# The dense tiles of each recurrent group: eight short pieces between the small steps instead of three blocks

## The chip, the cores and the metric

The kernel runs on one core of one Trainium2 chip. The metric is the device time of one execution in microseconds (us), taken as the median of the runs. The core's engines work side by side, each with a queue of its own, and are called here by their short names: PE (TensorE, matmuls; "PEld" is its weight load), DVE (VectorE), ACT (ScalarE), POOL (GpSimd) and SP (SyncE, which issues most of the transfers).

## The reference, cut to what matters

A decoder trunk of two layers, for a prompt of 256 tokens and 32 sample tokens (T = 288 together, all in float32). In each layer the mixer projects the normed input `u` with one wide weight and then runs a recurrence:

```python
z, xbc, dt_raw, q, k, v, g_ssd, g_attn = split_cols(u @ w_in, IN_SIZES)
...
y, new_ssm = ssd_scan(xs5, dt, a_head, bmat, cmat, ssm_state)   # 8 groups of 4 heads, head size 64, state size 128
y = grouped_rmsnorm(y.reshape(bsz, seqlen, D_INNER) * jax.nn.silu(z), ssd_norm, SSD_GROUPS)
ssd_out = y @ w_ssd_out
...
merged = jax.nn.sigmoid(g_ssd) * ssd_out + jax.nn.sigmoid(g_attn) * attn_out
```

The change touches only the stage in which `ssd_scan` is computed. The columns `z` (2048) and part of the gate columns `g_ssd` (1024) of the projection do not depend on the recurrence and are computed in the same stage.

## The kernel before, in words

Every float32 weight block is split in two parts. SP loads a unit of 256 columns (1 MB) into `raw` (two buffers), ACT writes its rounded copy `w_hi` (L672), DVE or, in this stage, POOL writes the rest `w_lo` (L1336), and `product` on PE makes each dense product from three matmuls of 288 columns (L1415 to L1417). A *step* below is one such call, that is one of the eight k blocks of a tile of 128 output columns; a *tile* is eight steps, 24 matmuls. A unit holds two tiles.

The recurrence runs over G = 8 groups in each of two layers, so 16 groups in all. What PE does in group g, in the order of its queue:

- turns of the group's x, B and C rows into bank 0, 1, 3 and 7 (L1516 with tile `flat`, L1772), which need `y_read` and `h_end_ready` of the group before; then `ssd_turned`
- the segment sums (L1779 to L1784), which need `a_tri_ready` of DVE; then `seg_product`
- one product for the middle state (L1790), which needs `xdt_ready` of DVE and `b_ready` of ACT; then **tile A**, `side(3g)`
- the y part (L1799 to L1813), which needs `m_ready`, DVE's last word on the decay matrices (L1250), and ends in `y_product`
- for t = 0 and t = 1: eight turns of a sample state (L1516 with tile `h`), then for t = 1 alone **tile B**, `side(3g + 1)`; then the pair L1832 (the new state, four matmuls of 512 columns with 32 rows) and L1836 (16 matmuls of 4 columns), of which L1836 needs `h0_t_ready` of ACT (L872), L1832 of t = 1 needs `h_new_ready` of DVE; then `h0_product`
- **tile C**, `side(3g + 2)`

The tiles of this stage share one bank of PSUM (`SIDE_BANK`), so the first step of a tile waits until ACT has copied the tile before it (`side_taken`). ACT follows in an order written out by hand: the copies of B (L853), the exponentials of the decays (L857 to L860), the copy of the middle state (L863), `side(3g)`, the final state (L868), the two state copies (L872), `side(3g + 1)`, `side(3g + 2)`. Its own `side(q)` (L842) waits for the tile, copies it out, takes the SiLU of a full pair of z tiles (L845, with a table load), and for odd q makes the `w_hi` of the unit after next. Whether q is odd depends on the group: tile B is the second of its unit in groups 0, 2, 4, 6 (the *even* groups) and makes a SiLU there too; A and C are second in the *odd* groups, and C has the SiLU.

DVE makes `a_tri` (L1207 to L1214), `xdt` and `xdte` (L1222 to L1235), `b_diag` (L1242), the decays (L1248, L1250), the y rows (L1255 to L1264), and after each `h0_product` eight updates of the state (L1271), then, after the second, `y_read` (L1282). POOL waits in its queue for `h_end_ready` and twice for `h_new_ready`, each time to write out a state; behind the second it makes a `w_lo` at the end of every group, and in odd groups another at the start, when tile A has set its `w_hi` free.

Of the kernel before, what the change touches and what calls it, by code (L numbers as in the profile page):

```python
# [25 lines left out]
KD = D // P  # L26
# [53 lines left out]
M_SIDE = M_XBC + PAIRS_XBC  # L80
# [103 lines left out]
def trunk(nc, x_prompt, x_sample, cache_kv_w128, cache_kv_w512, cache_kv_w2048, state_conv, state_ssm,  # L184
# [163 lines left out]
    with ExitStack() as ctx:  # L348
# [20 lines left out]
        lo_ready = [sem(f"lo_ready{s}", PAIRS, 1) for s in range(2)]  # L369
        unit_done = [sem(f"unit_done{s}", PAIRS, 1) for s in range(2)]  # L370
# [86 lines left out]
        side_first = sem("side_first", SIDE_TILES // 2)  # L457
        side_taken = sem("side_taken", SIDE_TILES)
# [23 lines left out]
        def wait(eng, signal, layer, n):  # L482

            eng.wait_ge(signal.sem, signal.at(layer, n))
# [178 lines left out]
        def _(act):  # L663
# [49 lines left out]
            with act.Fori(0, DEPTH) as l:  # L713
                m = l * PAIRS
# [48 lines left out]
                q = 0  # L763
                for _ in range(XBC_START):
                    q = xbc(q)
# [13 lines left out]
                for b in range(NB):  # L779
                    if b + 1 < NB:  # L780
                        key_tiles(b + 1)
                    for _ in range(XBC_KEYS[b]):
                        q = xbc(q)
# [5 lines left out]
                for _ in range(XBC_SOFTMAX[0]):  # L789
                    q = xbc(q)  # L790
# [3 lines left out]
                for _ in range(XBC_SOFTMAX[1]):  # L794
                    q = xbc(q)
# [5 lines left out]
                for _ in range(XBC_SOFTMAX[2] + sum(XBC_VALUES)):  # L801
                    q = xbc(q)
# [10 lines left out]
                for n in range(2 * HPG):  # L813
                    k = n % 2 + 1
# [35 lines left out]
                for g in range(G):  # L850
                    wait(act, ssd_turned, l, g + 1)
                    for c in range(2):
                        act.activation(b_tm[:, c, :], ps[:, 7, c * P:(c + 1) * P], ACT.Copy)  # L853
                    act.activation(b_tm_s[:], ps[0:TS, 7, 256:384], ACT.Copy).then_inc(b_ready.sem, 1)
                    wait(act, seg_product, l, g + 1)
                    for c in range(2):
                        act.activation(dec[c][:], ps[:, 4 + c, :].rearrange("p (h c) -> p h c", h=HPG), ACT.Exp)  # L857
                    act.activation(dec_s[:], ps[0:TS, 6, 336:464].rearrange("p (h c) -> p h c", h=HPG), ACT.Exp)
                    act.activation(e_off[:], ps[:, 6, 0:256].rearrange("p (t c) -> p t c", t=2), ACT.Exp)
                    act.activation(e_s[:], ps[:, 6, 256:336].rearrange("p (t c) -> p t c", t=2), ACT.Exp)\  # L860
                        .then_inc(dec_ready.sem, 1)
                    wait(act, h_mid_product, l, g + 1)
                    act.activation(h_mid[:], ps[:, 7, 0:256], ACT.Copy).then_inc(h_mid_ready.sem, 1)  # L863
                    side(3 * g)
                    wait(act, y_product, l, g + 1)
                    if g:
                        wait(act, h_end_out, l, 16 * g)
                    act.activation(h_end[:], ps[:, 7, 256:512].rearrange("p (t n) -> p t n", t=2), ACT.Copy)\  # L868
                        .then_inc(h_end_ready.sem, 1)
                    for t in (2 * g, 2 * g + 1):  # L870
                        wait(act, h0_turned, l, t + 1)
                        act.activation(h0_t[:], ps[:, 4:6, :].rearrange("p k (b c) -> p (k b) c", c=P), ACT.Copy)\  # L872
                            .then_inc(h0_t_ready.sem, 1)
                    side(3 * g + 1)
                    side(3 * g + 2)


                wait(act, z_used, l, G)
# [532 lines left out]
        def _(pe):  # L1411
# [128 lines left out]
            with pe.Fori(0, DEPTH) as l:  # L1540
# [202 lines left out]
                    last.then_inc(tails_turned.sem, 1)  # L1743


                def side(q):
                    n, s, half = q // 2, q // 2 % 2, q % 2
                    if q:
                        wait(pe, side_taken, l, q)
                    if not half:  # L1750
                        pe.wait_ge(lo_ready[s].sem, m + (M_SIDE + n // 2 + 2))
                    for k in range(KD):
                        last = product(ps[:, SIDE_BANK, 0:T], s, k * 256 + half * P, u_hi[:, k, :], u_lo[:, k, :],
                                       k == 0, k == KD - 1)
                    last.then_inc(unit_done[s].sem if half else side_first.sem, 1)

                wait(pe, xbc_ready, l, XBC_UNITS)
                wait(pe, tails_copied, l, 8)
                for g in range(G):
# [5 lines left out]
                    for c in range(3):  # L1765
# [5 lines left out]
                        turn(ps[0:n, 7, c * P:(c + 1) * P], fb[:, cols])  # L1771
                        last = pe.matmul(ps[0:n, 3, c * P:c * P + n], fb[:, cols], fc[:, cols], start=True, stop=True)  # L1772
                    last.then_inc(ssd_turned.sem, 1)

                    wait(pe, a_tri_ready, l, g + 1)
                    if g:
# [5 lines left out]
                    for t in range(2):  # L1782
                        pe.matmul(ps[:, 6, t * P:(t + 1) * P], a_exp[:, t * P:(t + 1) * P], tri, start=True, stop=True)
                        last = pe.matmul(ps[:, 6, 256 + t * 40:256 + (t + 1) * 40], a_exp_s[:, t * P:(t + 1) * P],  # L1784
                                         tri_sel_s, start=True, stop=True)
                    last.then_inc(seg_product.sem, 1)

                    wait(pe, xdt_ready, l, g + 1)
                    wait(pe, b_ready, l, g + 1)
                    pe.matmul(ps[:, 7, 0:256], b_tm[:, 0, :], xdte[:, 0, :], start=True, stop=True)\  # L1790
                        .then_inc(h_mid_product.sem, 1)
                    side(3 * g)

                    wait(pe, m_ready, l, g + 1)
                    for c in range(2):
# [14 lines left out]
                    for t in range(2):  # L1810
                        out = ps[:, 7, 256 + t * P:256 + (t + 1) * P]
                        pe.matmul(out, xdte[:, 2, t * P:(t + 1) * P], b_tm[:, 0, :], start=True, stop=False)
                        last = pe.matmul(out, xdte[:, 1, t * P:(t + 1) * P], b_tm[:, 1, :], start=False, stop=True)  # L1813
                    last.then_inc(y_product.sem, 1)

                    wait(pe, b_diag_ready, l, g + 1)
                    for t in range(2):
# [4 lines left out]
                        for b in range(NB):  # L1822
                            last = turn(ps[:, 4 + b // 4, (b % 4) * P:(b % 4 + 1) * P], h0[tile % 3][:, b, :])
                        last.then_inc(h0_turned.sem, 1)
                        if t:
                            side(3 * g + 1)

                        wait(pe, h_end_ready, l, g + 1)
                        if t:
# [6 lines left out]
                            last = pe.matmul(ps[:, 3 - 2 * t, 320 + b * NT:320 + (b + 1) * NT], h0_t[:, b, :],  # L1836
                                             fc[:, TP + b * NT:TP + (b + 1) * NT], start=True, stop=True)
                        last.then_inc(h0_product.sem, 1)
                    side(3 * g + 2)

                wait(pe, y_read, l, G)
                wait(pe, h_new_ready, l, KI)
# [78 lines left out]
```

## Time and the profile before

| what | value |
|---|---|
| median of three runs | 2479.61 us (2478.8 to 2480.71) |
| span of the profiled execution | 2479.5 us |
| PE busy over the span | 2237.7 us (90%) |
| DVE, ACT, POOL busy | 1291.6, 985.0, 417.0 us |
| mean granted clock of TensorE | 0.920 of full speed |
| recurrent stage of the first layer | about 569 to 853 us |
| recurrent stage of the second layer | about 1784 to 2068 us |

The profiled execution is told by its span alone, from the first to the last instruction, which lies within 0.2 us of the median of the runs. In a timeline row the first number is the start in us from the start of the span and the second its length; matmuls of one line that follow each other are merged in one row (x8 is eight of them), and the next row's start tells best when they were through. What stands in brackets is the idle time of the engine before the row and what ended it.

### The profile page before, as it was taken

To read this page: it belongs to the slowest core of one execution; us is meant where nothing else is said; L and a number is where in the kernel's file an instruction comes from. 1 tells how busy PE (TensorE), PEld (TensorE's weight loads), DVE (VectorE), ACT (ScalarE), POOL (GpSimd) and SP (SyncE) were. 2 spreads that over 40 slices of the span, in tenths; PEclk is the share of its full clock that TensorE was granted. 3 is DMA by queue.
4 is the path that set the end of the run, shared out by engine and by line. 5 is a ranking of instruction groups with operands and counts; after the bars stand their busy time and mean duration, and the time that the engine had idled before them with its cause. 6 is when DMAs were issued, how large, how long until landed. Compare 5 with 4: busy or idle time off the path is not lost.

```text
span 2479.5 us, 38482 instructions
## 1 busy us (share of the span) xinstructions
PE 2237.7 (90%) x15036; PEld 2079.1 (84%) x15036; DVE 1291.6 (52%) x1936; ACT 985.0 (40%) x1121; POOL 417.0 (17%) x162
## 2 busy tenths in 40 slices
PE   7999899988898888899989989999798889869996
PEld 5999889976677788799889989898677778869996
DVE  3553546665656472454355453576665663544543
ACT  3552434253333432454255434343432334325532
POOL 2000002211222355200000000121122223640000
PEclk9999989789888889999999999897988889989998
DMA  7444543413433333344444437442233332434441
GB/s 200 160 165 139 177 149 123 132 52 103 123 92 105 96 103 126 124 158 152 155 129 159 160 120 206 137 132 84 84 99 98 105 115 71 150 107 141 162 157 65
DMA packets 258231, 317.05 MB, mean 128 GB/s; under 512 B 9070, under 2 KB 232846, under 8 KB 258010
## 3 DMA queue, kind: packets, MB, share of 16 engines
q1 hardware_dynamic: 249656, 287.92, 36.4%
q0 software_dynamic: 7776, 26.73, 3.6%
q8 instruction: 76, 1.25, 0.2%
q10 hardware_dynamic: 680, 0.80, 0.1%
q14 instruction: 43, 0.35, 0.0%
HBM read 291.44 MB, written 26.33 MB: 128 GB/s over the span
## 4 chain that ended last, share of the span: by engine, by line
PE 72%; DVE 11%; PEld 5%; ACT 4%; issue 3%; POOL 3%; DVEq 1%; DMA 1%; SPq 0%; PEldq 0%; ACTq 0%; POOLq 0%
PE ps L1415 18%; PE ps L1417 17%; PE ps L1416 17%; PE ps L1516 4%; POOL w_lo L1336 3%; PE ps L1836 2%; PE ps L1832 2%; ACT w_hi L672 2%; DVE a_tri L1207 2%; DVE w_lo L923 1%; PE ps L1779 1%; PEld ps L1415 1%; PEld ps L1691 1%; PE ps L1500 1%; PEld ps L1417 1%
## 5 line engine op out<-in xcount | busy, mean ns | idle before, releaser
L1415 PE MATMUL ps<-u_hi,w_hi 128*128 128x288 f32 x2736 | 866.5, 317 | 50.0 <-DVE u_lo L950 39.7
L1416 PE MATMUL ps<-u_lo,w_hi 128*128 128x288 f32 x2736 | 848.3, 310 | 0.0
L1417 PE MATMUL ps<-u_hi,w_lo 128*128 128x288 f32 x2736 | 845.1, 309 | 0.0
L672 ACT ACTIVATE w_hi<-w_raw 128x2048 fp32r<-128x2048 f32 x249 | 476.2, 1912 | 660.7 <-PE ps L1417 634.8
L923 DVE TENSOR_TENSOR w_lo<-w_raw,w_hi 128x2048 fp32r<-128x2048 f32 x172 | 394.3, 2292 | 547.2 <-ACT w_hi L672 547.1
L1415 PEld LDWEIGHTS ps<-u_hi,w_hi 128*128 128x128 f32 x2736 | 554.7, 203 | 57.3 <-issue 53.7
L1416 PEld LDWEIGHTS ps<-u_lo,w_hi 128*128 128x128 f32 x2736 | 555.8, 203 | 0.5
L1417 PEld LDWEIGHTS ps<-u_hi,w_lo 128*128 128x128 f32 x2736 | 554.8, 203 | 0.0
L1336 POOL TENSOR_TENSOR w_lo<-w_raw,w_hi 128x2048 fp32r<-128x2048 f32 x77 | 358.0, 4649 | 626.0 <-ACT w_hi L672 625.8
L1415 PE MATMUL ps<-h_hi,w_hi 128*128 (+1 forms) x704 | 209.2, 297 | 14.6 <-DVE w_lo L923 14.6
L1417 PE MATMUL ps<-h_hi,w_lo 128*128 (+1 forms) x704 | 207.9, 295 | 0.0
L1416 PE MATMUL ps<-h_lo,w_hi 128*128 (+1 forms) x704 | 207.8, 295 | 0.0
L1415 PEld LDWEIGHTS ps<-h_hi,w_hi 128*128 128x128 f32 x704 | 132.8, 189 | 17.4 <-DVE w_lo L923 11.5
L1373 POOL DMA_DIRECT2D out_dram<-kv_p x6 | 4.1, 680 | 850.0 <-DVE kv_s L1085 849.8
L1416 PEld LDWEIGHTS ps<-h_lo,w_hi 128*128 128x128 f32 x704 | 132.9, 189 | 0.0
L1417 PEld LDWEIGHTS ps<-h_hi,w_lo 128*128 128x128 f32 x704 | 132.7, 188 | 0.0
L1271 DVE SCALAR_TENSOR_TENSOR h<-h,e_s,ps 128x128 f32<-128x128 f32 x256 | 69.0, 341 | 113.1 <-PE ps L1836 112.4
L1106 DVE SCALAR_TENSOR_TENSOR acc<-flat,conv_wt,acc 128x312 f32<-128x312 f32 x192 | 104.4, 585 | 7.3
L1415 PE MATMUL ps<-y_hi,w_hi 128*128 128x288 f32 (+1 forms) x256 | 79.3, 310 | 9.7 <-POOL w_lo L1336 9.7
L672 ACT ACT_TABLE_LOAD x45 | 57.7, 1283 | 71.1 <-DMA w_raw<-in_ffn_w_dram 71.1
L1836 PEld LDWEIGHTS ps<-flat,h_t 128*128 128x128 f32 x512 | 60.7, 195 | 24.3 <-ACT h_t L872 12.1
L1416 PE MATMUL ps<-y_lo,w_hi 128*128 128x288 f32 (+1 forms) x256 | 77.9, 304 | 0.0
(270 smaller groups left out, 2803.6 us busy)
## 6 DMA issues: line engine op xcount, KB each, us to landing
w_raw<-in_ffn_w_dram SPq DMA_DIRECT2D x128, 1024.0 KB, 5.0
w_raw<-in_w_in_dram SPq DMA_DIRECT2D x82, 1024.0 KB, 5.3
h<-in_state_ssm_dram SPq DMA_DIRECT2D x32, 512.0 KB, 4.1
out_dram<-h POOLq DMA_DIRECT2D x32, 512.0 KB, 3.8
w_raw<-in_w_ssd_out_dram SPq DMA_DIRECT2D x16, 1024.0 KB, 4.9
kv_in<-in_cache_kv_w_dram SPq DMA_DIRECT2D x32, 256.0 KB, 4.1
w_raw<-in_w_o_dram SPq DMA_DIRECT2D x8, 1024.0 KB, 5.0
w_raw<-in_ffn_w_dram SPq DMA_DIRECT2D x8, 512.0 KB, 3.5
```

Source lines behind the costliest of these rows:

```text
L672: act.activation(w_hi[s][:], raw[s][:], ACT.Copy).then_inc(hi_ready[s].sem, 1)
L923: dve.tensor_tensor(w_lo[s][:], raw[s][:], w_hi[s][:].bitcast(F32), ALU.subtract)\
L1106: last = dve.scalar_tensor_tensor(out=dst, in0=src, scalar=tap, in1=dst, op0=ALU.mult, op1=ALU.add)
L1207: dve.tensor_scalar(a_tri[c][:, h, :], tri, da[:, c, HPG * g + h:HPG * g + h + 1], None, ALU.mult)
L1271: dve.scalar_tensor_tensor(out=h0[tile % 3][:, b, :], in0=h0[tile % 3][:, b, :], scalar=e_s[:, t, TS + b:TS + b + 1], in1=ps[:, 6 + b // 4 ...
L1336: pool.tensor_tensor(w_lo[s][:], raw[s][:], w_hi[s][:].bitcast(F32), ALU.subtract)\
L1415: pe.matmul(out, wh, hi, start=first, stop=False)
L1416: pe.matmul(out, wh, lo, start=False, stop=False)
L1417: return pe.matmul(out, wl, hi, start=False, stop=last)
L1516: return pe.transpose(out, src, square[0:p, 0, 0:p])
L1832: pe.matmul(ps[:, 6 + n, :], xdte_s[:, t * P:(t + 1) * P], b_diag[:, 4 * n:4 * n + 4, :].rearrange("p b n -> p (b n)"), start=True, stop=True)
L1836: last = pe.matmul(ps[:, 3 - 2 * t, 320 + b * NT:320 + (b + 1) * NT], h0_t[:, b, :], fc[:, TP + b * NT:TP + (b + 1) * NT], start=True, sto ...
```

## The change

PE's `side(q)`, which issued a whole tile, becomes `fill(at, steps)`, which issues the next `steps` steps, wherever they lie in their tiles, with the same waits in front of a tile's first step and the same signals behind its last. PE calls it eight times in a group, with 3, 2, 3, 3, 2, 3, 3 and 5 steps. Tile A is 3 + 2 + 3, tile B 3 + 2 + 3, and tile C 3 + 5. On ACT, `side(3g + 1)` and `side(3g + 2)` move: the first now stands between the two state copies, the second still behind both. No instruction is added or removed on any engine, and SP's, POOL's and DVE's queues stay as they are.

```diff
@@ ACT, in group g
                     for t in (2 * g, 2 * g + 1):
                         wait(act, h0_turned, l, t + 1)
                         act.activation(h0_t[:], ps[:, 4:6, :].rearrange("p k (b c) -> p (k b) c", c=P), ACT.Copy)\
                             .then_inc(h0_t_ready.sem, 1)
-                    side(3 * g + 1)
-                    side(3 * g + 2)
+                        side(t + g + 1)
@@ PE
-                def side(q):
-                    n, s, half = q // 2, q // 2 % 2, q % 2
-                    if q:
-                        wait(pe, side_taken, l, q)
-                    if not half:
-                        pe.wait_ge(lo_ready[s].sem, m + (M_SIDE + n // 2 + 2))
-                    for k in range(KD):
-                        last = product(...)
-                    last.then_inc(unit_done[s].sem if half else side_first.sem, 1)
+                def fill(at, steps):
+
+                    for i in range(at, at + steps):
+                        q, k = divmod(i, KD)
+                        n, s, half = q // 2, q // 2 % 2, q % 2
+                        if k == 0 and q:
+                            wait(pe, side_taken, l, q)
+                        if k == 0 and not half:
+                            pe.wait_ge(lo_ready[s].sem, m + (M_SIDE + n // 2 + 2))
+                        last = product(ps[:, SIDE_BANK, 0:T], s, k * 256 + half * P, u_hi[:, k, :], u_lo[:, k, :],
+                                       k == 0, k == KD - 1)
+                        if k == KD - 1:
+                            last.then_inc(unit_done[s].sem if half else side_first.sem, 1)
+                    return at + steps
...
                     last.then_inc(ssd_turned.sem, 1)
+                    filled = fill(filled, 3)
...
                     last.then_inc(seg_product.sem, 1)
+                    filled = fill(filled, 2)
...
                         .then_inc(h_mid_product.sem, 1)
-                    side(3 * g)
+                    filled = fill(filled, 3)
...
                     last.then_inc(y_product.sem, 1)
+                    filled = fill(filled, 3)
...
                         last.then_inc(h0_turned.sem, 1)
-                        if t:
-                            side(3 * g + 1)
+                        filled = fill(filled, 3 if t else 2)
...
                         last.then_inc(h0_product.sem, 1)
-                    side(3 * g + 2)
+                        filled = fill(filled, 5 if t else 3)
```

## Rows read from the trace of the kernel before

**Rows 1.** Windows view: busy time and instructions of each engine, granted clock, DMA.

```profile
565.00:865.00 300.00, 265.60 (x1631) 216.62 (x1632) 173.59 (x453) 108.34 (x172) 78.96 (x39) 0.88 0.34 102
...
778.00:778.50 0.50, 0.50 (x4) 0.50 (x4) 0.50 (x3) 0.00 (x0) 0.00 (x0) 0.50 0.00 0
```

**Rows 2.** Waits of PE, 565 to 865 us: total, times, longest.

```profile
PE ps L1779 <- DVE a_exp_s L1214: 14.0, 4, 4.4
PE ps L1799 <- DVE dec_s L1250: 6.4, 2, 3.2
```

**Rows 3.** Timeline of group 1, an odd group, from tile C of group 0.

```profile
595.42 0.38 PE L1415 MATMUL ps<-u_hi,w_hi 128*128 128x288 f32 x1
...
598.57 6.76 DVE L1207 TENSOR_SCALAR a_tri<-square,da 128x128 f32<-128x128 f32 x8
...
599.34 4.53 POOL L1336 TENSOR_TENSOR w_lo<-w_raw,w_hi 128x2048 fp32r<-128x2048 f32 x1
...
606.37 3.68 PE L1779 MATMUL ps<-a_tri,square 128*128 128x512 f32 x4 [4.39 <-DVE a_exp_s L1214]
...
611.49 0.41 PE L1784 MATMUL ps<-small,a_exp_s 32*128 32x40 f32 x2
...
614.79 0.27 DVE L1250 TENSOR_TENSOR dec_s<-dec_s,cbm_s 32x128 f32<-32x128 f32 x1
...
615.63 1.09 PE L1799 MATMUL ps<-dec,xdt 128*64 128x128 f32 x16
...
618.45 1.04 PE L1516 MATMUL ps<-square,h 128*128 128x128 f32 x8
...
623.13 1.59 PE L1516 MATMUL ps<-square,h 128*128 128x128 f32 x8
...
628.89 1.98 PE L1832 MATMUL ps<-b_diag,xdte_s 32*128 32x512 f32 x4
...
632.60 0.38 PE L1415 MATMUL ps<-u_hi,w_hi 128*128 128x288 f32 x1
```

**Rows 4.** Timeline of group 6, an even group, from tile C of group 5.

```profile
776.59 0.38 PE L1415 MATMUL ps<-u_hi,w_hi 128*128 128x288 f32 x1
...
781.39 0.49 PE L1516 MATMUL ps<-square,flat 128*128 128x128 f32 x3
...
785.92 5.45 POOL L1336 TENSOR_TENSOR w_lo<-w_raw,w_hi 128x2048 fp32r<-128x2048 f32 x1 [5.03 <-ACT w_hi L672]
...
793.91 1.74 PE L1799 MATMUL ps<-dec,xdt 128*64 128x128 f32 x16 [3.18 <-DVE dec_s L1250]
...
798.28 1.04 PE L1516 MATMUL ps<-square,h 128*128 128x128 f32 x8
...
803.79 0.38 PE L1415 MATMUL ps<-u_hi,w_hi 128*128 128x288 f32 x1
...
804.07 1.03 ACT L872 ACTIVATE h_t<-ps 128x1024 f32<-128x1024 f32 x1 [3.69 <-PE ps L1516]
...
807.15 1.98 PE L1832 MATMUL ps<-b_diag,xdte_s 32*128 32x512 f32 x4
...
809.06 1.95 PE L1836 MATMUL ps<-flat,h_t 128*128 128x4 f32 x16
...
809.62 1.90 ACT L672 ACTIVATE w_hi<-w_raw 128x2048 fp32r<-128x2048 f32 x1
...
810.87 0.38 PE L1415 MATMUL ps<-u_hi,w_hi 128*128 128x288 f32 x1
```

**Rows 5.** Timeline of group 4, an even group whose `xdt` is late.

```profile
711.79 4.50 POOL L1336 TENSOR_TENSOR w_lo<-w_raw,w_hi 128x2048 fp32r<-128x2048 f32 x1 [3.90 <-ACT w_hi L672]
...
717.29 1.22 PE L1790 MATMUL ps<-xdte,b_tm 128*128 128x256 f32 x2 [3.47 <-DVE xdte_s L1235]
...
720.17 0.27 DVE L1250 TENSOR_TENSOR dec_s<-dec_s,cbm_s 32x128 f32<-32x128 f32 x1
```

**Rows 6.** Timeline where the stage ends, first dense matmul of the gates.

```profile
853.69 0.40 PE L1415 MATMUL ps<-u_hi,w_hi 128*128 128x288 f32 x1 [0.85 <-ACT silu_z L842]
```

More of the change, by code:

```diff
@@ L1743, in _ @@
                     last.then_inc(tails_turned.sem, 1)
-                def side(q):
-                    n, s, half = q // 2, q // 2 % 2, q % 2
-                    if q:
-                        wait(pe, side_taken, l, q)
-                    if not half:
-                        pe.wait_ge(lo_ready[s].sem, m + (M_SIDE + n // 2 + 2))
-                    for k in range(KD):
+                def fill(at, steps):
[6 more added lines that the diff above has]
+                            pe.wait_ge(lo_ready[s].sem, m + (M_SIDE + n // 2 + 2))
                         last = product(ps[:, SIDE_BANK, 0:T], s, k * 256 + half * P, u_hi[:, k, :], u_lo[:, k, :],
                                        k == 0, k == KD - 1)
-                    last.then_inc(unit_done[s].sem if half else side_first.sem, 1)
+                        if k == KD - 1:
+                            last.then_inc(unit_done[s].sem if half else side_first.sem, 1)
+                    return at + steps
+                filled = 0
                 wait(pe, xbc_ready, l, XBC_UNITS)
```

## The prediction, made before the changed kernel ran

> **What bounds the kernel now.** The busy shares come first, in the windows view of the first recurrent stage: PE is busy 265.60 of 300 us, DVE 173.59, ACT 108.34 [rows 1]. So the stage is PE's, less about 34 us in which PE waits, and the granted clock is 0.88, because in part of the time PE runs at the lower of its two levels, 1.2 instead of 2.4 GHz (0.50 in the second row). The view of PE's waits says who holds it up: 14.0 us in four waits for `a_tri`, 6.4 us in two for `m_ready` [rows 2]. The timelines say why. In an odd group DVE starts `a_tri` 3.15 us after tile C has begun, but POOL's `w_lo` of 4.53 us starts 0.8 us later and the eight small DVE instructions take 6.76 us, so L1779 begins 10.95 us after C [rows 3]. In an even group POOL's `w_lo` begins 4.5 us after C's end, and PE then waits 3.18 us for `m_ready` [rows 4] or 3.47 us for `xdt_ready` [rows 5]. The cause of each long wait is thus where `w_lo` meets DVE, and that is the first thing to ask of the change: does it move the waits, or fill them?
>
> I measure each group from its mark, the first matmul of the tile C before it. An odd group lasts 632.60 - 595.42 = 37.2 us [rows 3], an even one 810.87 - 776.59 = 34.3 us [rows 4].
>
> **Prices.** A tile at full clock takes 807.15 - 803.79 = 3.36 us [rows 4]: 0.40 us a step and about 0.16 us for going in and out. So pieces of 2, 3 and 5 steps cost 0.95, 1.35 and 2.15 us. With a stretch at 1.2 GHz a tile took 781.39 - 776.59 = 4.8 us [rows 4]. Five more pieces a group cost 0.8 us where PE does not wait anyway.
>
> **The boundary to an odd group (8 groups): nothing.** Before, PE has eight steps between the mark and L1779, all in C. After, it has 5 of C and 3 of A: eight again. `a_tri` does not hang on them: the `w_lo` that delays it is released by `h_new_ready`, which follows the mark. Five steps (2.2 to 3.3 us), the wait for `y_read` at 3.15, turns of 1.8 and three steps end at 6.3 to 7.3 us, and L1779 starts at 10.95 as before. The 4.4 us wait isn't filled by anything that was not done there before.
>
> **The rest of an odd group.** Seg ends at +16.4 (L1784) and `m_ready` comes at +19.6 [rows 3]. PE now has only 2 + 3 steps and L1790 to fill that: 16.4 + 0.95 + 0.4 + 1.35 = 19.1, a new wait of 0.5 us; before, the eight steps ran to +20.2 and hid it. The y part takes 618.45 - 615.63 = 2.8 us [rows 3]. Then 3 steps 1.35, turns 1.0, 2 steps 0.95, the pair L1832 and L1836 3.8 us (a bit over twice 1.9 [rows 4]), 3 steps 1.35, turns 0.85, 3 steps 1.35, the pair 3.7: 19.6 + 0.1 + 2.8 + 14.4 = 36.9 us at full clock. Before, the part from the second turns to L1832 took 628.89 - 623.13 = 5.8 us [rows 3], against 0.85 + 3.36 = 4.2 in group 6: 1.6 us lost to the half clock that followed the first pair. The pair stays whole in the change, so I expect the fall to come in about seven of ten groups: + 1.15, or 38.05 us against 37.2. Sum for eight: +7 us; bounds -2 (no fall) and +11 (always).
>
> **An even group behind an odd one (6 groups).** C now ends 2.2 to 3.0 us after the mark instead of 4.8, so ACT's `w_hi` and POOL's `w_lo`, 4.5 us behind it, start at +6.7 to +7.5, not +9.3. That turns these groups into group 4's kind: `xdt_ready` 1.0 us and `m_ready` 4.15 us behind the end of `w_lo` [rows 5], that is at +12.6 and +15.8. PE: `y_read` 3.15, turns 1.75, 3 steps 1.35, seg 3.85, 2 steps 0.95: at +11.1 it waits 1.5 us, does L1790 and 3 steps until +14.4, waits 1.4, and starts y at +15.8 instead of +17.3, but three steps behind. The y part took 4.4 us behind its 3.2 us wait (798.28 - 793.91 [rows 4]) and 2.8 in group 1; I take 3.6. With the three steps the next point of equal work is at +20.75, against +21.7 before: 0.9 us gained. Then a new wait. ACT's `side(3g + 1)` now stands ahead of the second state copy, and in even groups it brings the copy, the SiLU with its table load and a `w_hi`: from B's end at 807.15 to 809.62 + 1.90 is 4.4 us [rows 4], and L872 adds 1.03. So `h0_t_ready` comes 5.5 us behind B's end, while PE needs it after turns 0.85, 3 steps 1.35 and L1832 1.9, at 4.1: 1.4 us of waiting. Before, ACT did L872 first and had B's work done behind it, hidden. Three more pieces add 0.45 and the half clock, which partly hides in that wait, 0.3 on average. Together +1.2 us against rows 4; group 4 itself is 0.7 us longer already. Sum for six: +6 us; bounds -4 and +14.
>
> **Group 0 of each layer (2).** It has no C before it, and the change moves three steps of C in front of its end (1.35). It takes the 1.4 us wait for `h0_t`, about 0.9 at `m_ready` and 0.45 of pieces: +4 us each, +8 us.
>
> **The end of each layer (2).** C has five steps left there, not eight, and the first dense matmul of the gates followed it directly, behind 0.85 us for `side_taken` [rows 6]; `y_read` at +3.15 is next. So -1.9 us each, -4 us; a `w_lo` that is released by C's end comes as much earlier.
>
> **Other queues.** The weight transfers wait for `w_lo` and `h_new_out`; a piece that begins earlier needs only weights that were ready a group before. No transfer becomes a term; it would cost the whole stall of ACT if `raw` were not there for the `w_hi` now ahead of L872, but that load was issued behind the states of the group before, over 15 us ahead. Sum: 7 + 6 + 8 - 4 = +17 us on the profiled 2479.5, which is the median too: 2496 us.
>
> **A rule of the skill against this change.** Here full clock held through the undivided tile at 803.79 and half clock was granted at 778, shortly behind a pair [rows 1, 4]. The Trainium skill's "TensorE: Matmul & The Clock Gate", section "A second HAM failure mode: psum-queue depth-cycling", says that frequent small gaps between groups of matmuls make the clock swing between its two levels. No row here tells whether short pieces do that. By the rule the sum would be the third rival's, by the rows it is the one above.
>
> **Rivals.** (1) *Held clock, faster.* Dense steps between the turns and the pairs keep the engine active, so it no longer falls behind the pair or behind the 4.4 us wait. For: it falls now behind the longest stretch without dense work. Without falls the odd groups give -2, the even ones about 0, the first and last +4; and L1779, which takes 3.6 us behind the wait [rows 3] and could take 1.9, gives 8 x 1.7 = -14. That is 2468 us. It decides from the point where L1779 runs at full clock in most odd groups. Against: 4 us of idling are left in front of it. Chance 0.15. (2) *A wash.* The new waits hide in half-clock stretches and the falls become fewer behind the pair, L1779 stays slow: +2 us, 2481 us. Chance 0.18. (3) *More falls.* Each of 16 groups gets one more stretch at 1.2 GHz for 1.6 us: +26 on my sum, 2522 us; half of that is 2509. Chance 0.15. (4) My forecast, 2486 to 2507: chance 0.52.
>
> **How the numbers follow.** The predicted time is (4)'s. The range goes from rival 1's end to the middle of rival 3, 2470 to 2516 us. 0.2% is 5 us, about what a measurement of this kernel can tell from no change. Faster by more than that: rival 1 and a little of 2, 0.18. Within it: 0.16. Slower: 0.66.
>
> **What the profile after would show.** Step by step: L1779's wait for `a_tri` in odd groups unchanged near 4 us; waits for `xdt_ready` and `m_ready` of 1 to 2 us in even groups and of 0.5 in odd ones; a new wait of L1836 for ACT's L872 near 1.4 us in the eight even groups; no wait of a piece for `side_taken` or `w_lo`; dense matmuls of 0.44 us in about as large a share as now. The forecast is wrong if the wait for L872 is missing, if L1779 takes 1.98 us in odd groups, or if PE's clock in the stage leaves 0.86 to 0.90.

## The result and the profile after

The changed kernel is slower: the ratio of its time to the time before is 1.0165, with a 95% interval from 1.0152 to 1.0178. That is 41 us on 2480 us, so about 2521 us; I had forecast 2496 us and a range up to 2516. The ratio leaves out one of five executions of either kernel, 3529.72 us at a granted clock of 0.553 for the changed one, which was also the profiled one, and 5215.91 us for the one before, so the rows below come from a second profiled execution of the changed kernel (2522.73 us, span 2519.6 us).

The windows view of the first recurrent stage, with the columns of [rows 1]:

```profile
565.00:865.00 300.00, 271.62 (x1504) 224.77 (x1505) 165.75 (x430) 94.19 (x158) 69.79 (x35) 0.80 0.32 97
```

The two recurrent stages whole, from their first turn to the first dense matmul of the gates, the kernel before first:

```profile
569.29:853.69 284.40, 255.91 (x1561) 207.11 (x1561) 170.98 (x441) 93.00 (x154) 72.60 (x37) 0.87 0.34 103
1784.44:2068.64 284.20, 255.56 (x1561) 207.51 (x1561) 170.97 (x441) 92.89 (x154) 73.56 (x37) 0.88 0.34 103
568.51:876.82 308.31, 281.99 (x1561) 233.45 (x1561) 169.29 (x441) 93.62 (x154) 71.37 (x37) 0.80 0.31 93
1804.16:2109.05 304.89, 277.68 (x1560) 228.85 (x1561) 168.66 (x441) 93.52 (x154) 70.89 (x37) 0.81 0.32 94
```

PE's waits over the whole span, with their sum in us, their number and the longest, three kinds before and the same three after:

```profile
PE ps L1779 <- DVE a_exp_s L1214: 27.2, 7, 4.4
PE ps L1799 <- DVE dec_s L1250: 15.9, 5, 3.2
PE ps L1790 <- DVE xdte_s L1235: 3.5, 1, 3.5
...
PE ps L1784 <- DVE a_exp_s L1213: 19.7, 6, 3.5
PE ps L1805 <- DVE dec_s L1249: 12.1, 13, 1.3
PE ps L1796 <- DVE xdte_s L1234: 9.1, 6, 1.5
```

PE issued 1504 matmuls in the 300 us instead of 1631, and yet it was busy longer, 271.62 us against 265.60: the granted clock is 0.80, against 0.88 in [rows 1]. The whole stages say it more plainly. The same 1561 matmuls kept PE busy for 281.99 instead of 255.91 us in the first stage, and the two stages together grew by 44.6 us. The waits did not grow. L1784, which was L1779, waited up to 3.5 us for `a_tri` where it waited 4.4 [rows 2], and the three kinds of wait shown add up to 40.9 us over the kernel, against 46.6 before. All of PE's waits add up to 232.0 us, against 235.6, while its busy time over the span rose from 2237.7 to 2281.2 us.

The timeline of group 6 of the changed kernel answers to [rows 4]; L1805 is the y part, L1838 and L1842 are the pair that was L1832 and L1836:

```profile
797.87 0.59 PE L1414 MATMUL ps<-u_hi,w_hi 128*128 128x288 f32 x1
...
805.57 1.88 PE L1784 MATMUL ps<-a_tri,square 128*128 128x512 f32 x4
...
811.83 0.70 PE L1796 MATMUL ps<-xdte,b_tm 128*128 128x256 f32 x2 [1.52 <-DVE xdte_s L1234]
...
815.04 1.10 PE L1805 MATMUL ps<-dec,xdt 128*64 128x128 f32 x16 [1.32 <-DVE dec_s L1249]
...
820.81 1.98 PE L1838 MATMUL ps<-b_diag,xdte_s 32*128 32x512 f32 x4
822.72 2.38 PE L1842 MATMUL ps<-flat,h_t 128*128 128x4 f32 x16
824.96 0.59 PE L1414 MATMUL ps<-u_hi,w_hi 128*128 128x288 f32 x1
825.82 0.44 PE L1414 MATMUL ps<-u_hi,w_hi 128*128 128x288 f32 x1
826.54 0.44 PE L1414 MATMUL ps<-u_hi,w_hi 128*128 128x288 f32 x1
827.26 1.91 PE L1515 MATMUL ps<-square,h 128*128 128x128 f32 x8
828.82 0.59 PE L1414 MATMUL ps<-u_hi,w_hi 128*128 128x288 f32 x1
...
831.12 1.98 PE L1838 MATMUL ps<-b_diag,xdte_s 32*128 32x512 f32 x4
833.03 2.45 PE L1842 MATMUL ps<-flat,h_t 128*128 128x4 f32 x16
835.34 0.59 PE L1414 MATMUL ps<-u_hi,w_hi 128*128 128x288 f32 x1
```

From mark to mark (797.87 to 835.34) the group lasts 37.5 us instead of 34.3. Read the lengths. Two of the waits that I had forecast are there, 1.52 for 1.5 and 1.32 for 1.4. At 822.72, the first L1842, 24.9 us have passed since the mark. From there to the end of the group dense matmuls take 0.44 us instead of 0.29, the eight turns 1.91 instead of 1.07, and the sixteen matmuls of four columns 2.38 and 2.45 instead of 1.95. The clock falls before the first pair has ended, the three steps behind it run at 1.2 GHz, so do the turns and nearly all of the next three steps. L1838 of the second pair is back at 1.98 us, and this pair brings the next fall.

How long the lower level lasts behind the second pair is the difference to before. The windows view of group 6, the kernel before in the first two rows, the changed one in the last three (the clock is the third number from the end):

```profile
811.00:814.50 3.50, 3.50 (x17) 3.50 (x17) 3.18 (x14) 0.52 (x1) 0.00 (x0) 0.54 0.52 150
814.50:818.00 3.50, 2.93 (x24) 2.58 (x23) 3.50 (x3) 0.94 (x4) 3.35 (x2) 0.98 0.50 150
...
834.00:837.50 3.50, 3.50 (x18) 3.50 (x18) 1.99 (x8) 0.00 (x0) 0.00 (x0) 0.54 0.48 143
837.50:841.00 3.50, 3.50 (x18) 3.48 (x17) 3.23 (x9) 0.41 (x1) 1.89 (x2) 0.50 0.12 36
841.00:844.50 3.50, 2.23 (x16) 1.70 (x15) 3.50 (x1) 1.87 (x4) 3.50 (x1) 0.98 0.39 114
```

In the same view in windows of 0.5 us, both stages of the kernel before hold 38 stretches below full clock, which add up to 140 us at the lower level, 3.7 us each on average. Those of the changed kernel hold 36, which add up to 242 us, 6.7 us each. So the clock does not fall more often; it stays down longer.

### The profile page after: what moved, and what is told of

The parts are those of the page before. It is cut to its first block, busy times and chain, and to the rows that moved or that the text cites. A ratio compares the mean times of both kernels' runs of the same rounds, so it can differ in the third digit from the quotient of the medians.

```text
span 3526.5 us, 38482 instructions
## 1 busy us (share of the span) xinstructions
PE 3364.8 (95%) x15036; PEld 2939.8 (83%) x15036; DVE 1260.0 (36%) x1936; ACT 987.1 (28%) x1121; POOL 409.7 (12%) x162
## 4 chain that ended last, share of the span: by engine, by line
PE 81%; PEld 10%; DVE 4%; issue 2%; ACT 1%; DMA 1%; DVEq 0%; POOL 0%; PEldq 0%; SPq 0%; ACTq 0%
PE ps L1414 21%; PE ps L1415 21%; PE ps L1416 20%; PE ps L1515 3%; PE ps L1842 3%; PE ps L1838 3%; PEld ps L1414 2%; PEld ps L1416 2%; PEld ps L1415 2%; PE ps L1784 1%; PE ps L1499 1%; PEld ps L1690 1%; PEld ps L1636 1%; DVE a_tri L1206 1%; PE ps L1492 1%
## 5 line engine op out<-in xcount | busy, mean ns | idle before, releaser
L1414 PE MATMUL ps<-u_hi,w_hi 128*128 128x288 f32 x2736 | 1147.8, 420 | 46.6 <-DVE u_lo L949 39.8
L1415 PE MATMUL ps<-u_lo,w_hi 128*128 128x288 f32 x2736 | 1122.0, 410 | 0.0
L1416 PE MATMUL ps<-u_hi,w_lo 128*128 128x288 f32 x2736 | 1121.3, 410 | 0.0
L1414 PEld LDWEIGHTS ps<-u_hi,w_hi 128*128 128x128 f32 x2736 | 653.5, 239 | 92.3 <-issue 53.0
L1415 PEld LDWEIGHTS ps<-u_lo,w_hi 128*128 128x128 f32 x2736 | 655.1, 239 | 34.3
L1416 PEld LDWEIGHTS ps<-u_hi,w_lo 128*128 128x128 f32 x2736 | 653.9, 239 | 33.5
L1415 PE MATMUL ps<-h_lo,w_hi 128*128 (+1 forms) x704 | 278.6, 396 | 0.0
L1842 PEld LDWEIGHTS ps<-flat,h_t 128*128 128x128 f32 x512 | 110.0, 327 | 47.9 <-issue 47.9
L1842 PE MATMUL ps<-flat,h_t 128*128 128x4 f32 x512 | 112.8, 352 | 0.0
L1838 PE MATMUL ps<-b_diag,xdte_s 32*128 32x512 f32 x128 | 106.1, 973 | 0.0
L1416 PE MATMUL ps<-y_hi,w_lo 128*128 128x288 f32 (+1 forms) x256 | 104.2, 407 | 0.0
```

Source lines behind the costliest of these rows:

```text
L1414: pe.matmul(out, wh, hi, start=first, stop=False)
L1415: pe.matmul(out, wh, lo, start=False, stop=False)
L1416: return pe.matmul(out, wl, hi, start=False, stop=last)
L1838: pe.matmul(ps[:, 6 + n, :], xdte_s[:, t * P:(t + 1) * P], b_diag[:, 4 * n:4 * n + 4, :].rearrange("p b n -> p (b n)"), start=True, stop=True)
```

## The experiments

All compare with the kernel before, run beside each of them on the same chip. The schedule stands for the steps at the eight places: behind the turns, behind seg, behind L1790 | behind y, behind the turns of t = 0, behind its pair, behind the turns of t = 1, behind its pair. Before it is 0, 0, 8 | 0, 0, 0, 8, 8; the change is 3, 2, 3 | 3, 2, 3, 3, 5. Clock is that of the windows view from 565 to 865 us; PE's busy time and the sum of its waits are those of the whole span. These three come from the one profiled execution, which is not always near the median: that of b_moved took 2530.2 us, the longest of its five (2499.87 to 2530.2), and that of y_to_pair 2480.09 us. All kernels but filler3 issue the same 15036 matmuls, so a longer busy time is the same work done more slowly.

| run | schedule | ACT's order | ratio (95%) | median us | clock | PE busy us | PE's waits us |
|---|---|---|---|---|---|---|---|
| before | 0, 0, 8 / 0, 0, 0, 8, 8 | old | 1 | 2480 | 0.88 | 2237.7 | 235.6 |
| changed | 3, 2, 3 / 3, 2, 3, 3, 5 | new | 1.0165 (1.0152 to 1.0178) | about 2521 | 0.80 | 2281.2 | 232.0 |
| a_split | 3, 2, 3 / 0, 0, 0, 8, 8 | old | 0.998 (0.9971 to 0.999) | 2477.16 | 0.87 | 2238.8 | 231.1 |
| bc_split | 0, 0, 8 / 3, 2, 3, 3, 5 | new | 1.0109 (1.0089 to 1.013) | 2507.63 | 0.85 | 2248.4 | 250.6 |
| act_old | 3, 2, 3 / 3, 2, 3, 3, 5 | old | 1.0368 (1.0323 to 1.0414) | 2575.94 | 0.77 | 2307.2 | 258.0 |
| b_cut | 0, 0, 8 / 0, 0, 4, 4, 8 | old | 0.999 (0.998 to 0.9999) | 2478.0 | 0.88 | 2235.7 | 231.8 |
| b_moved | 0, 0, 8 / 5, 0, 0, 3, 8 | old | 1.0095 (1.0078 to 1.0112) | 2508.37 | 0.80 | 2293.5 | 228.3 |
| c_whole | 3, 2, 3 / 3, 2, 0, 3, 8 | old | 1.0278 (1.0256 to 1.0299) | 2548.96 | 0.77 | 2317.9 | 224.0 |
| y_to_gap | 3, 2, 3 / 0, 0, 8, 3, 5 | new | 1.0125 (1.0094 to 1.0155) | 2512.42 | 0.82 | 2266.9 | 239.3 |
| gap_first | 3, 2, 3 / 0, 0, 8, 0, 8 | old | 0.9996 (0.9986 to 1.0006) | 2480.07 | 0.87 | 2242.4 | 231.2 |
| end_short | 3, 2, 3 / 0, 0, 0, 11, 5 | old | 1.0131 (1.0114 to 1.0148) | 2513.43 | 0.84 | 2263.9 | 242.7 |
| filler3 | as changed, plus added work | new | 1.0182 (1.0165 to 1.0199) | 2524.92 | 0.88 | 2277.6 | 237.3 |
| y_to_pair | five steps in pair 0 | new | 1.004 (1.0012 to 1.0068) | 2490.27 | 0.87 | 2230.1 | 240.6 |
| pair_cut | steps in both pairs | old | 0.993 (0.9913 to 0.9946) | 2464.71 | 0.93 | 2205.4 | 251.0 |
| only_low | as before, POOL's order | old | 0.9806 (0.978 to 0.9831) | 2435.33 | 0.91 | 2217.2 | 212.5 |
| pair_low | as pair_cut, POOL's order | old | 0.9699 (0.9682 to 0.9717) | 2406.63 | 0.95 | 2182.2 | 218.7 |

**Waits or clock.** First the changed kernel again, for its profile, and its halves apart.

> The changed kernel once more, for a profile at an undisturbed clock. The change costs about 41 us on the timed runs, of which I had forecast 17. Theory W (waits): the new waits are larger than I took them, so waits of PE in the two recurrent stages add up to 40 us more than before and the stage's granted clock stays near 0.88. Theory C (clock): the waits are as forecast or smaller, and some 25 us or more come from dense matmuls at 1.2 GHz; then the clock of the stage falls to 0.80 or less and the share of dense matmuls at the longer spacing rises from about 27% to over 40%.

It took 2522.73 us. The clock was 0.80 and the waits were smaller, so theory W fell. Of the dense matmuls of both stages, 49% start 0.19 us or more ahead of the next one, against 30% before. All of the growth of the span is busy time: 43.5 us more, with 3.6 us less of waiting.

```diff
# a_split, against the changed kernel: A in pieces, B and C whole; ACT's order as before (not shown)
-                    filled = fill(filled, 3)      # behind the y part
...
-                        filled = fill(filled, 3 if t else 2)
+                        filled = fill(filled, 8 if t else 0)      # behind the turns
...
-                        filled = fill(filled, 5 if t else 3)
+                        filled = fill(filled, 8 if t else 0)      # behind the pair
# bc_split, against the changed kernel: only B and C in pieces, ACT's new order
-                    filled = fill(filled, 3)      # behind the turns
-                    filled = fill(filled, 2)      # behind seg
-                    filled = fill(filled, 3)      # behind L1790
+                    filled = fill(filled, 8)      # behind L1790
```

> Only tile A is divided (3 + 2 + 3), B and C stay whole and ACT keeps its order of before. Theory W: the m_ready wait of 0.5 us in odd groups and less cover in even ones, no wait for L872: within 5 us of before. Theory C says that each block that is cut up costs clock: +10 to +15 us if cutting A matters as much as cutting B and C, about 0 if only the pieces around the pairs L1832 and L1836 matter.

> Only tiles B and C are divided, with ACT's new order; A stays whole behind L1790. Theory W: the wait for L872 in eight even groups, 1.4 us each, and three more steps in front of the end of group 0: +15 us. Theory C: most of the 41 us, +30 or more, with more dense matmuls at 1.2 GHz behind the pairs.

Dividing A gains 3.9 us; dividing B and C costs 27 us. That is short of theory C's 30 us and over theory W's 15, and the profile has both: 15.0 us more of waits than before and 10.7 us more of busy time. The split of B and C also shows the wait that I had looked for; its clock of 0.85 is higher than the 0.80 of the changed kernel. PE's waits of bc_split over its whole span:

```profile
PE ps L1783 <- DVE a_exp_s L1213: 34.4, 10, 5.6
PE ps L1794 <- DVE xdte_s L1234: 20.8, 6, 3.7
PE ps L1840 <- ACT h_t L872: 8.1, 8, 1.1
```

Eight waits for ACT's second state copy, one in each even group, 1.0 us each.

```diff
# act_old: the changed kernel with ACT's order as before
-                        side(t + g + 1)
+                    side(3 * g + 1)
+                    side(3 * g + 2)
```

> All pieces of the change on PE, but ACT copies both states before it turns to tiles B and C, as before. Theory W: L1836's wait for L872 goes, but tile C's first step at t = 1 now waits for ACT to copy the second state (1.03 us) and tile B (0.41 us), some 0.7 us in all 16 groups: within 8 us of the changed kernel. Theory C: also within 8 us of the changed kernel, since the pieces lie where they lay. If ACT's order were the main cost, this would stand 15 us or more below it.

A miss: it stood 53 us above the changed kernel's 2522.73. PE's queue shows half of why. The first step of C, issued behind the turns of t = 1, waits for ACT to take B, and ACT is in the state copy: waits for `side_taken` (in the list, ACT silu_z L842) are 24.6 us in 18 over the whole span, up to 1.5 us each, where the kernel before has 1.7 us in 2. All waits together are 26.0 us longer than in the changed kernel, and the busy time is longer by another 26.0 us. So about half of the miss is waits and half is clock.

**What lets the clock fall.** Is it the cutting, or where the steps lie?

```diff
# b_cut and b_moved, as compared with the kernel before; A whole behind L1790, ACT's order as before
# b_cut
+                        filled = fill(filled, 4 if t else 0)      # behind the turns
...
+                        filled = fill(filled, 8 if t else 4)      # behind the pair
# b_moved
+                    filled = fill(filled, 5)                      # behind the y part
...
+                        filled = fill(filled, 3 if t else 0)      # behind the turns
...
+                        filled = fill(filled, 8 if t else 0)      # behind the pair
```

> The kernel before with one cut: four steps of tile B ahead of the second turns and four behind them; A and C whole, ACT's order as before. All amounts of work between two small steps stay, only the eight steps lie in two halves around 0.85 us of turns. If cutting by itself lets the clock fall (fragments), +10 us or more. If it is the amount of dense work between one pair (L1832 and L1836) and the next, which stays at eight steps: within 5 us of before.

> The kernel before with five steps of tile B ahead of the first turns, behind the y part, and only three left between the first pair and the second; A and C whole. If the amount between the pairs decides, the clock falls in most groups as in the changed kernel and L1836 of the second pair takes 2.6 us: +15 to +30 us. If fragments decide, there is one more piece only: +5 us at most.

Cutting B in place costs nothing (2.9 us faster than before). Moving five of its steps from between the pairs to ahead of the first costs 28 us, with as many pieces as b_cut has. So it is not the fragments. (The clock of 0.80 in the table is that of its slowest execution.)

Next, single moves of the changed kernel's pieces, and added work:

```diff
# filler3: in the changed kernel, in front of the second half of each L1838
                         for n in range(2):
+                            for k in range(6 * n):
+                                pe.matmul(ps[:, 7, 0:T], u_hi[:, k, 0:P], u_hi[:, k, :], start=True, stop=True)
                             pe.matmul(ps[:, 6 + n, :], xdte_s[:, t * P:(t + 1) * P],
# y_to_pair, against the changed kernel: the five steps ahead of the first pair go between L1838 and L1842
-                    filled = fill(filled, 3)                      # behind the y part
-                        filled = fill(filled, 3 if t else 2)
+                        filled = fill(filled, 3 if t else 0)
+                        filled = fill(filled, 0 if t else 5)      # within the pair
# y_to_gap, against the changed kernel: the same five go behind the first pair
-                    filled = fill(filled, 3)
+                        filled = fill(filled, 3 if t else 0)
+                        filled = fill(filled, 5 if t else 8)
```

> The changed kernel with added work: six more dense matmuls of 288 columns in the middle of each L1832, into a bank that L1832 then overwrites; they change no result. They cost 0.8 us each time at 2.4 GHz, 32 times 0.8 = 26 us. Theory W: 26 us or more above the changed kernel. Theory C: the work holds the clock in part of the groups, and the time rises by less than 15 us or falls, with a granted clock above 0.903.

> The changed kernel with one thing moved: the five steps of tile B that it issues ahead of the first pair (3 behind the y part, 2 behind the first turns) stand in one piece between L1832 and L1836 of that pair. Theory C, in the form that the fall comes where a pair follows or precedes too little dense work: most of the 41 us go, 2485 us or less, and the stage's clock is back at 0.88 or above. Theory W: the waits stay what they are, within 8 us of the changed kernel's 2521.

> The changed kernel with the same five steps behind the first pair, so that eight steps of B follow it directly and three of C follow the second turns: eleven steps between the pairs. If the amount between the pairs decides, as the runs that cut B in place (no loss) and moved five steps forward (+27 us) suggest: most of the 41 us go too, 2490 us or less. If only work inside a pair helped, it stays above 2505.

The added work of filler3 in the second pair of group 1, L1840 and L1844 being the pair here:

```profile
632.86 1.12 PE L1840 MATMUL ps<-b_diag,xdte_s 32*128 32x512 f32 x2
633.91 1.07 PE L1839 MATMUL ps<-u_hi 128*128 128x288 f32 x6
634.90 1.12 PE L1840 MATMUL ps<-b_diag,xdte_s 32*128 32x512 f32 x2
635.96 1.95 PE L1844 MATMUL ps<-flat,h_t 128*128 128x4 f32 x16
```

From the start of L1840 to that of L1844 it is 3.10 us, and without the added six it is 1.91 (831.12 to 833.03 above). That is 1.19 us at each of 32 places, 38 us in all and more than the 26 that I had reckoned. The kernel took about 4 us longer than the changed one (the intervals of the two ratios overlap): the added work bought back nearly all of its time, and the clock rose from 0.80 to 0.88. This is the plainest sign that the clock, and not the work or the waits, is what the change costs.

Five steps moved into the first pair took the 41 us down to 10 us, short of the 2485 us or less expected. Its eight waits of 1.3 us for ACT's L872 do not explain that by themselves, since the profiled execution has them and took 2480.09 us. The move behind the pair missed: 2512 us.

```diff
# all three have A in 3 + 2 + 3 and ACT's order as before; each line stands for the call at its place
# gap_first: nothing behind the y part
+                        filled = fill(filled, 0)                  # behind the turns
+                        filled = fill(filled, 8)                  # behind either pair
# end_short: nothing behind the y part
+                        filled = fill(filled, 11 if t else 0)     # behind the turns
+                        filled = fill(filled, 5 if t else 0)      # behind the pair
# c_whole
                     filled = fill(filled, 3)                      # behind the y part
                         filled = fill(filled, 3 if t else 2)      # behind the turns
+                        filled = fill(filled, 8 if t else 0)      # behind the pair
```

> Tile A in 3 + 2 + 3, tile B whole directly behind the first pair, C whole at the end, ACT's order as before, so that no wait for ACT's second state copy falls into the second pair. If that wait (with what it does to the clock) was y_to_gap's trouble: near the run that divided A alone, 2477 us, within 8 us. If B ahead of the turns is itself bad: 2500 us or more.

> Tile A in 3 + 2 + 3, eight steps of B and three of C in one piece behind the second turns, five of C at the end, ACT's order as before. PE waits about 0.5 us in each group for ACT to take tile B, 8 us in all. If five instead of eight steps behind the second pair let the clock fall: 2500 us or more and a stage clock under 0.85. If not: 2477 + 8 = 2485 us, clock 0.87 or above.

> The changed kernel with C whole at the end and ACT's order as before: A 3 + 2 + 3, B 3 + 2 ahead of the first pair and 3 behind it, eight steps behind the second. It has neither the wait for ACT's second copy nor a short end. If the five steps ahead of the first pair, and so only three between the pairs, are what costs the clock: 2500 us or more, near the run that moved them alone (2508). If it is the wait or the short end: 2485 us or less.

With eight steps behind each pair the time is that of before (gap_first). end_short differs from a_split only in that three steps of C stand ahead of the second pair, so that five instead of eight follow it. It takes 34 us more than the kernel before, of which 7 us are waits by the table (those for `side_taken` are 8.3 us in 16, against 1.7 in 2). A short end alone thus costs as much as y_to_gap lost; what y_to_gap's eight waits for L872 (10.2 us) did there was not taken apart. With five ahead of the first pair and three between the pairs, it is 69 us more (c_whole), although PE waits less there than in the kernel before: all its waits over the whole span add up to 224.0 us, against 235.6. Three rows of that view of c_whole:

```profile
PE ps L1806 <- DVE dec_s L1250: 24.3, 15, 3.2
PE ps L1785 <- DVE a_exp_s L1214: 14.9, 6, 2.7
PE ps L1516 <- DVE flat L1282: 6.2, 2, 3.2
```

In its timeline the whole second pair of group 2 runs at the lower level. The four matmuls of L1839 (L1832 before) take 3.78 instead of 1.98 us and the sixteen of L1843 (L1836 before) 3.58 instead of 1.95:

```profile
676.98 3.78 PE L1839 MATMUL ps<-b_diag,xdte_s 32*128 32x512 f32 x4
680.68 3.58 PE L1843 MATMUL ps<-flat,h_t 128*128 128x4 f32 x16
```

**Versions that beat the kernel before.** The pair is the weak place, so I put pieces inside it.

```diff
# pair_cut: A in 3 + 2 + 3, ACT's order as before
                         for b in range(NB):
                             last = turn(ps[:, 4 + b // 4, (b % 4) * P:(b % 4 + 1) * P], h0[tile % 3][:, b, :])
                         last.then_inc(h0_turned.sem, 1)
+                        filled = fill(filled, 4 if t else 0)
...
                             pe.matmul(ps[:, 6 + n, :], xdte_s[:, t * P:(t + 1) * P], ...)
+                        filled = fill(filled, 3 if t else 4)      # within the pair
                         wait(pe, h0_t_ready, l, tile + 1)
...
                         last.then_inc(h0_product.sem, 1)
+                        filled = fill(filled, 5 if t else 0)
```

> Pieces within the pairs: tile A 3 + 2 + 3 as in the run that divided A alone, four steps of B between L1832 and L1836 of the first pair, four behind the second turns, three steps of C between L1832 and L1836 of the second pair, five at the end. If the 3.8 us of a pair, in which the array has little to do, are what brings the clock down, it stays up in most groups and the kernel beats the one before by 10 us or more (2465 us). If fragments decide, the time lies 15 us or more above before.

2464.71 us, with a clock of 0.93, although PE's waits are longer now (251.0 us against 235.6; a `y_read` wait of 1.05 us at twelve of the fourteen boundaries between groups is new). The other cause of idle time, the `w_lo` at the boundary, was put to the test by POOL's order alone:

```diff
# only_low (on the kernel before) and pair_low (on pair_cut)
                     for t in (2 * g, 2 * g + 1):
+                        if t % 2 and g % 2 == 0:
+                            side_low((3 * g + 1) // 2 + 2)
                         wait(pool, h_new_ready, l, t + 1)
...
-                    side_low((3 * g + 1) // 2 + 2)
+                    if g % 2:
+                        side_low((3 * g + 1) // 2 + 2)
```

> The kernel before with POOL's order alone changed in the same way. ACT has the w_hi that it needs ready 0.6 us behind the mark there, so w_lo runs from +0.6 to +5.2, y_read waits for it until +5.4, and L1779 starts at +8.4 instead of +10.95: 8 times 2.5 = 20 us faster. No change if w_lo does not set a_tri's time.

> The run with pieces inside the pairs (2465 us), and POOL's w_lo at the end of even groups placed ahead of its wait for the second h_new_ready instead of behind it. The 4.4 us wait of L1779 in the eight odd groups was laid to this w_lo, which holds DVE's a_tri up. Then w_lo runs while DVE updates the state from PSUM, a_tri comes some 3.5 us earlier and the kernel gains 8 times 3 to 3.7 = 24 to 30 us: 2437 us. If the wait had another cause, or only moved elsewhere, within 8 us of 2465.

Both gained more than expected: 45 us on the kernel before (23.1 us less of waits and 20.5 us less of busy time), and 58 us on pair_cut, to 2406.63 us, 3.0% below the kernel before. The timeline of only_low at the boundary that [rows 3] show before:

```profile
595.46 2.15 DVE L1271 SCALAR_TENSOR_TENSOR h<-h,e_s,ps 128x128 f32<-128x128 f32 x8 [6.96 <-PE ps L1839]
...
596.01 4.55 POOL L1336 TENSOR_TENSOR w_lo<-w_raw,w_hi 128x2048 fp32r<-128x2048 f32 x1 [6.76 <-ACT w_hi L672]
...
598.26 2.35 DVE L1282 SCALAR_TENSOR_TENSOR flat<-flat,skip,off_s 128x32 f32<-128x32 f32 x1
...
600.53 1.82 DVE L1207 TENSOR_SCALAR a_tri<-square,da 128x128 f32<-128x128 f32 x8
...
603.39 1.98 PE L1782 MATMUL ps<-a_tri,square 128*128 128x512 f32 x4 [0.89 <-DVE a_exp_s L1214]
```

`w_lo` now holds up only one small instruction, L1282, which takes 2.35 us where it took 0.25; the eight `a_tri` take 1.82 us instead of 6.76. PE waits 0.89 us instead of 4.39, and L1782 (L1779 before), with only short idle time ahead of it, takes 1.98 instead of 3.68 us, which is the part that my expectation left out. The Trainium skill's "SBUF — State Buffer", section "Who interferes with whom", says that GpSimd and VectorE share one pair of ports, and that the instruction that starts first holds it while the other stands still, and that this holds for a VectorE instruction with two inputs in SBUF beside a GpSimd instruction that reads SBUF. The trace agrees: `w_lo` started at 596.01 and ended at 600.56, L1282 has two such inputs and stood from 598.26 to about 600.6, while the state updates (L1271), with one input in PSUM, kept their 2.15 us for eight.

## Why the prediction was wrong, point by point

- **The sign was right, the size was not**: +17 us forecast, +41 us measured. The waits and the end were sized well. The term that failed is the half clock.
- **Boundary to an odd group, "nothing"**: right. Where the trace has the wait for `a_tri`, in six of the eight odd groups, it is 3.0 to 3.5 us, behind eight steps as before; in group 1 L1784 starts 11.0 us behind the mark (600.48 to 611.44), as it did before.
- **New waits**: `xdt_ready` 1.52 (1.5 forecast), `m_ready` 1.32 (1.4) in even groups, 0.6 (0.5) in odd ones. All three were there.
- **ACT's second state copy in even groups**: the mechanism was right. In group 6 B ends at 827.2 and the copy (831.66, 1.00 us long) at 832.7, so 5.5 us, as forecast. But PE's list of waits has none for it in the changed kernel, where half clock had used up nearly all of the time first (L1842 starts at 833.03). It stands in the list at 1.0 us in bc_split and 1.3 in y_to_gap and y_to_pair. That this wait was missing was one of my three signs of being wrong, and the clock outside 0.86 to 0.90 was another; both came. The third, L1779 at full speed in odd groups, came in part: L1784 took under 2 us in four of the eight.
- **The end of each layer**: 1.9 us less forecast. Measured from mark to the gates' first matmul, 876.8 - 873.1 = 3.7 us for 5.8, so 2.1 less.
- **The half clock, "+1.15" in an odd group and "0.3 on average" in an even one**: this is the step that failed. The table has the two stages from mark to mark.

| term | forecast us | measured us, both stages |
|---|---|---|
| odd groups (8) | +7 | +22.1 |
| even groups behind an odd one (6) | +6 | +15.0 |
| group 0 of each layer (2) | +8 | +11.7 |
| the end of each layer (2) | -4 | -4.2 |

They sum to 44.6 us, which is the growth of the two stages; the whole span grew by 40.1, so a few microseconds came back elsewhere. I had assumed that the pair, being untouched, would bring the clock down as before, in seven of ten groups, and for one stretch that costs 1.6 us. No row that I show gives seven of ten. The turns of t = 1, which take 1.07 us at full clock, tell of it: before they took 1.32 us or more in eight of sixteen groups, in the changed kernel 1.91 us in fifteen and 1.31 in the last one. And the stretches grew longer, from 140 to 242 us in all, as shown above. I had priced the turns and the pair at full clock throughout. Of the 43.5 us more of busy time, 16.6 lie in the matmuls of four columns (63.5 us before, 80.1 after) and 7.9 in the turns of the states (38.6 and 46.5).
- **What I had moved**: the pair was untouched, but not what stands around it. Between the pairs stand six steps, three on either side of the turns, instead of eight; behind the second pair five instead of eight. Shown by the runs: with eight between the pairs and eight behind the second nothing is lost (b_cut, a_split), nor with eight directly behind each pair (gap_first). With only three between the pairs it costs 28 us (b_moved), with only five behind the second 27 us besides the waits (end_short), and with work inside both pairs the clock is better than it was in the kernel before (0.93, pair_cut). The prices do not add: the changed kernel, which has both faults, loses 41 us, and c_whole, which has only the first in a stronger form, 69.
- **My rival 3, "more falls"**, had the right cause and the wrong form. It gave each group one more half-clock stretch, 1.6 us. The stretches were not more but longer. That its time, 2522 us, is nearly the one measured is partly luck: it put 26 us to the clock, where PE's busy time rose by 43.5, and the rest of its sum, which is mine, to new waits and pieces, where the waits in all did not rise. The section "A second HAM failure mode: psum-queue depth-cycling" of the Trainium skill's "TensorE: Matmul & The Clock Gate", which stood beside that rival, speaks of frequent small idle gaps between groups of matmuls. Here the idle time did not grow (232.0 us of waits against 235.6), and in b_cut the cut of a tile in two cost nothing, so it is neither the gaps nor the number of pieces.

What stays open: why act_old and c_whole fall as far as they do. c_whole has three dense steps between the pairs and act_old six around a wait, and in c_whole the lower level lasts through the second pair itself. But b_moved, also with three between the pairs, lost less than half of what c_whole did. Nor does any run vary the number of steps by ones, so how many are enough is not shown. That y_to_pair ranges from 2478.43 to 2507.88 us over eight executions and b_moved from 2499.87 to 2530.2 over five, wider than any other, was not explained either.

## What to carry to other kernels

Before dense work is spread as filler, list what the engine does at low activity (here a 3.8 us pair of thin matmuls, with 32 rows or four columns) and keep a full block, here eight steps, between one such stretch and the next, or put work into the middle of it; an even spread with unbroken thin stretches can cost more than the waits that it fills. Compare the engine's busy time for the same instructions, before and after: here that told clock from waits at a glance. Filler that only passes from one side of a wait to the other fills nothing: count the steps between the event that releases the late one and the wait, before and after. Where POOL and DVE meet, ask which order of POOL's queue puts its long instruction beside DVE work that has an input in PSUM; here that one move was worth 45 us on the kernel before.

## What the runs showed of the hardware beyond what I expected

- The four-column matmuls are not free of the clock: sixteen take 1.95 us at 2.4 GHz and 3.58 us at 1.2 GHz (granted clock 0.50 from 677 to 684.3 us in c_whole), though each has only four columns.
- Useless dense work can nearly pay for itself: 192 added matmuls, which took up 38 us, cost 4 us.
- The clock can fall within the thin pair, with PE busy and before the next dense matmul: L1842 took 2.38 us against 1.95.
- A worse clock need not mean more falls: 36 stretches at the lower level instead of 38, but 242 us instead of 140.
